# A hybrid encoder layer on one core: square sums spread between dense matmul steps, four small moves beside it

## The chip, the core and the metric

The kernel runs on one core of a Trainium2 chip. A core has a matmul engine (TensorE, PE in the profile), a vector engine (VectorE, DVE), an activation engine (ScalarE, ACT), GpSimd (POOL), and a queue engine that starts DMAs (SyncE, SP). Each runs its own list of instructions in order, and they wait for one another through semaphores. On-chip memory is SBUF; TensorE writes to PSUM, which has eight banks here. The metric is the device time of one execution in microseconds (us); lower is better.

## The reference

One layer (DEPTH = 1) of a streaming encoder is applied to a prompt of 1024 frames and to 32 further frames of another stream, 1024 channels wide, all in 32-bit floats:

```
xn = rmsnorm(x, g_mix)
u_lru, y_lru, q, k, v, gates = split(xn @ w_in)
xc = causal_dwconv(u_lru)                   # width 4
h  = rg_lru(xc)                             # two block-diagonal gates, then a scan over positions
br_lru  = (h * gelu(y_lru)) @ w_br_lru
q, k = rmsnorm(q per head, g_q), rmsnorm(k per head, g_k)
br_attn = attention(q, k, v, sink) @ w_br_attn   # chunks of 64 frames, own chunk and 2 before it
g = sigmoid(gates + b_gate)
x = x + (g0 * br_lru + g1 * br_attn) @ w_out
gate_pre, up = split(rmsnorm(x, g_ffn) @ w_up)
x = x + (gelu(causal_dwconv(gate_pre)) * up) @ w_down
```

Outputs are x for both streams and the states: last inputs of the convolutions, last h, last keys and values.

## The kernel before

Activations lie transposed, channels on the 128 partitions and the T = 1056 frames (1024 + 32) along the free dimension, as KT = 8 rows of 128 channels. The frames are cut into three chunks of 352. A dense product (`chunk`) is a run of 8 **steps**, one for each k; a step is three matmuls of 128x352 (high part of the weights by high part of the data, high by low, low by high: three passes in a fast format stand for one in full precision). A tile is 3 chunks by 8 steps, 72 matmuls. Tiles go in pairs, X in PSUM banks 0 to 2 with weight slot 0 and Y in banks 3 to 5 with slot 1. SyncE loads the next 512 KB of weights when a tile is done, and GpSimd splits them into high and low parts. The order of the work on each engine is written out by hand, so TensorE's list below is the program's.

The stages in order: the norm and the first tiles; keys; values; attention, in two halves of 17 blocks (the 16 chunks of frames and the sample's); attention's output product; the recurrent part (`PAIR_R`), one row of 128 channels for each turn of a loop; the gated product with its result (`PAIR_G0`); the output product; the feed-forward part in three thirds; the stores of the result.

*Keys and values.* Heads are normalised by the sums of squares over 64 channels. For keys, `key_sum` is a matmul of 128x352 in full precision into bank 6 or 7, and ScalarE takes the root (`key_root`, L892). There are six of them, two rows by three chunks, placed in `keys_between` among the steps of a query tile. Values are computed by frames, in nine tiles of 128 frames (`v_half`), each in two halves of 4 steps, whose matmuls are 128x256. Only tiles 0 to 5 have a bank at once; 6 to 8 take the banks of 0 to 2 when ScalarE has copied those out (`v_out`, L896). Queries of two tiles are copied and squared by ScalarE in `last_queries` (L883, L884) while the values are computed.

*Queries' square sums.* `query_sums(a, b)` computes for one half a (0 or 1) the sums of a chunk of frames b: one or two units, and each unit is a full-precision matmul with a 128x128 piece of squares as the stationary operand and a moving operand of 2 columns (L526). A half has 33 units, and the profile records each as two instructions. Half 0 is done in three groups of 12, 12 and 9 units behind the first halves of value tiles 6, 7 and 8 (`SUMS_AT`), half 1 in three groups of the same sizes in attention blocks 13, 14 and 15, between `scores` and `product`.

*Attention.* Block g on TensorE is `scores(g + 1)` (L549), `product(g - 1)` (L575), `transposes(g)` (L560) and then some steps of a dense tile that has nothing to do with it (`fill`): a query tile of half 1, then from block 12 on tiles of the attention's gate, 7 steps for a block. ScalarE does the exponentials (L910), VectorE the maxima, the scaling (L1298), and the copies.

*Recurrent part and what follows it.* For a row j, `lru_gates(j, n)` are two full-precision matmuls of chunk n (L715, L716). ScalarE makes them decays (L1047 to L1054), VectorE scans over the frames and leaves the result of a row as c_hi, d_lo. The last row's three `lru_gates` stand in and before the Y tile of pair `PAIR_G0`. Then comes the X tile of pair `PAIR_G0 + 1`, which multiplies all eight rows by w_br_lru, and which waits at its last step (k = 7) of each chunk for the last row. VectorE joins a finished chunk of it with the gate in GG (L1470, L1473), and ScalarE puts the next gate into GG (L1008), which frees the bank of the Y tile.

*The end.* The last dense tile adds to `resid` (L1569), and SyncE stores each row of 128 channels once its three chunks are done (L396): eight stores of 528 KB, one for each row.

Of the kernel before, what the change touches and what calls it, by code (L numbers as in the profile page):

```python
# [122 lines left out]
def build(nc, xT, W, wab, vecs, mats, kc, vc, yT, o_lconv, o_h, o_fconv, o_kp, o_ks, o_vp, o_vs):  # L123
    ctx = ExitStack()
    with ctx:
# [204 lines left out]
        SUMS_AT = {NB - 4: range(0, 6), NB - 3: range(6, 12), NB - 2: range(12, NB)}  # L330
# [35 lines left out]
        def _(sp):  # L366
# [64 lines left out]
        def _(pe):  # L431
# [29 lines left out]
            def last_row(sem_, value):  # L461
# [4 lines left out]
                return before  # L466
# [43 lines left out]
            def v_half(tt, s):  # L510

                t0 = tt * P if tt < SEQ // P else T - P
                to = bank[tt % 6]
                for k in range(4 * s, 4 * s + 4):
                    for j, (w, x) in enumerate(((w_hi, x_hi), (w_hi, x_lo), (w_lo, x_hi))):
# [4 lines left out]
            def query_sums(a, b):  # L520

                for u in range(units_of(b)):
                    t0 = SMP if b == NC else b * CHUNK + u * DSEQ
                    sq = q_sq[a][:, t0:t0 + DSEQ, :].rearrange("p t r -> p (t r)")
                    at = SUMS_COL[a] + 2 * (2 * b + u)
                    last = nc.tensor.matmul(bank[SUMS_BANK[a]][:, at:at + 2], sq, bones[:, 0:P:HD], start=True, stop=True)  # L526
                if b == NC:
                    last.then_inc(a_qs, 1)
# [50 lines left out]
            def beside(s, p, n, ks):  # L579
# [10 lines left out]
                chunk(s, n, x_hi, x_lo, to=n, ks=ks)  # L590

            def fill(work):
                for (s, p, n), ks in work:
                    beside(s, p, n, ks)

# [40 lines left out]
            key_sum(1, 2)  # L636

            pe.wait_ge(wx_ready, PAIR_V + 1)
            for tt in range(6):
                pe.wait_ge(*((x_act, out_before(2) + tt + 1) if tt < 3 else (y_act, out_before(2) + tt - 2)))  # L640
                v_half(tt, 0)
            pe.wait_ge(wy_ready, PAIR_V + 1)
            for tt in range(3):
                v_half(tt, 1).then_inc(v_done, 1)
            pe.wait_ge(h_rt, 6)
            for tt in range(6, 9):
                pe.wait_ge(v_free, tt - 5)
                v_half(tt, 0).then_inc(x_done, 1)
                if tt == 6:
                    pe.wait_ge(h_sqd, 12)  # L650
                for b in SUMS_AT[tt - 6 + NB - 4]:
                    query_sums(0, b)
# [13 lines left out]
            fill(fill_of(0)[1:])  # L666
            for g in range(1, BLOCKS):
# [4 lines left out]
                if g in SUMS_AT:  # L672
                    pe.wait_ge(x_act, out_before(PAIR_G))
                    pe.wait_ge(y_act, out_before(PAIR_G))
                    for b in SUMS_AT[g]:
                        query_sums(1, b)
                product(g - 1)
                transposes(g)
                fill(fill_of(g))
# [11 lines left out]
            def gated(p0, stage, between=None, second=None, before=None):  # L691
# [4 lines left out]
                if between is not None:  # L696
                    between()
                tile(1, 0, p0, x_hi, x_lo, y_act, ya, before=second)
                pe.wait_ge(x_act, xa + 3)
                if before is not None:  # L700
                    pe.wait_ge(r_lo, START + 3 * (KT - 1))
                tile(0, 0, p0 + 1, c_hi, d_lo, before=before)
# [23 lines left out]
            def gates_first():  # L726
                pe.wait_ge(s_wab, 16 * KT)
                lru_gates(KT - 1, 0)

            def gates_later(n, k):  # L730
                if (n, k) in ((0, KT // 2), (1, 0)):
                    lru_gates(KT - 1, n + 1)


            gated(PAIR_G0, "G0", gates_first, gates_later, last_row(r_lo, START + 3 * (KT - 1)))


# [56 lines left out]
        def _(act):  # L794
# [882 lines left out]
```

## Time and profile before

| | |
|---|---|
| median of 3 runs | 1806.59 us (1802.4, 1808.53, 1806.59) |
| profiled execution, its time | 1809.89 us |
| its span in the trace | 1808.1 us |
| TensorE busy | 1794.6 us, 99% of the span |
| VectorE, ScalarE, GpSimd busy | 838.0, 561.4, 499.8 us |
| mean DMA rate | 49 GB/s |

The span is what the trace covers from the first instruction to the last; the execution's own time is 1.8 us more. A busy TensorE is not one at its peak: its instructions are counted as busy whatever they do and at whatever clock. The page's row PEclk shows the clock that TensorE was granted in 40 equal slices, in tenths.

### The profile page before, as it was taken

The page shows a single profiled execution, that of the slowest core. Times are in us where ns is not written, and L with a number is a line of the kernel's source. Part 1 is how long each engine was busy: PE and PEld are TensorE (multiplying, and loading weights), DVE is VectorE, ACT ScalarE, POOL GpSimd, SP SyncE. Part 2 cuts the span into 40 slices and gives each one's busy share as a digit, 9 for nine tenths or more (in the row PEclk, how much of TensorE's full clock was granted, in tenths as well). Part 3 has the DMA queues.
Part 4 walks back from the last instruction along what each step waited for, and adds up shares of the span by engine and source line. Part 5 has one row for each costly group of instructions (what it writes and reads, how often), then busy time and mean ns, then how long its engine had stood idle before and what let it go on. Part 6 is the DMA issues. An engine that isn't in the chain of part 4 may idle for free.

```text
span 1808.1 us, 29895 instructions
## 1 busy us (share of the span) xinstructions
PE 1794.6 (99%) x11252; PEld 1746.7 (97%) x11252; DVE 838.0 (46%) x1624; ACT 561.4 (31%) x1117; POOL 499.8 (28%) x282
## 2 busy tenths in 40 slices
PE   9999999999999999999999999999999999999999
PEld 8998888899999999999999999999999999999999
DVE  7946757711247676112465555411555511555511
ACT  5535544400156765112133332200322300333300
POOL 3112101122332232333332333332223333333222
PEclk9989989999999999999999999999999999999999
DMA  4011000011111111111311111111111111111113
GB/s 162 25 30 42 24 24 24 24 50 46 39 47 41 52 38 38 47 46 46 143 47 36 46 46 46 47 46 47 46 46 42 41 46 46 46 46 46 46 46 121
DMA packets 28514, 89.16 MB, mean 49 GB/s; under 512 B 3472, under 2 KB 8496, under 8 KB 28464
## 3 DMA queue, kind: packets, MB, share of 16 engines
q1 hardware_dynamic: 25200, 82.49, 13.7%
q10 hardware_dynamic: 3264, 5.96, 1.0%
q8 instruction: 37, 0.61, 0.1%
q14 instruction: 13, 0.11, 0.0%
HBM read 83.70 MB, written 4.73 MB: 49 GB/s over the span
## 4 chain that ended last, share of the span: by engine, by line
PE 95%; DVE 2%; ACT 2%; issue 0%; DMA 0%; SPq 0%; ACTq 0%; DVEq 0%
PE banks L440 85%; PE banks L560 2%; PE banks L575 2%; PE banks L516 1%; PE banks L549 1%; PE banks L526 1%; PE banks L716 1%; PE banks L715 1%; DVE x_lo L1198 1%; DMA resid<-xT 0%; DVE x_lo L1183 0%; DVE resid L1191 0%; ACT prB L910 0%; DVE merged L1206 0%; DVE prB L1298 0%
## 5 line engine op out<-in xcount | busy, mean ns | idle before, releaser
L440 PE MATMUL banks<-x_hi,w_hi 128*128 128x352 f32 x1752 | 578.5, 330 | 4.6 <-DVE x_lo L1183 3.1
L440 PE MATMUL banks<-x_hi,w_lo 128*128 128x352 f32 x1752 | 568.5, 324 | 0.0
L440 PE MATMUL banks<-x_lo,w_hi 128*128 128x352 f32 x1752 | 566.8, 324 | 0.0
L409 POOL TENSOR_SCALAR w_hi<-w_raw 128x1024 fp32r<-128x1024 f32 x137 | 157.0, 1146 | 1238.4 <-DMA w_raw<-W 1238.4
L440 PE MATMUL banks<-h_hi,w_lo 128*128 128x352 f32 x1152 | 372.7, 323 | 0.0
L440 PE MATMUL banks<-h_hi,w_hi 128*128 128x352 f32 x1152 | 372.4, 323 | 0.0
L440 PE MATMUL banks<-h_lo,w_hi 128*128 128x352 f32 x1152 | 371.6, 323 | 0.0
L440 PEld LDWEIGHTS banks<-x_hi,w_hi 128*128 128x128 f32 x1752 | 331.6, 189 | 9.0 <-issue 3.1
L411 POOL TENSOR_TENSOR w_lo<-w_raw,w_hi 128x1024 fp32r<-128x1024 f32 x137 | 334.1, 2439 | 11.4
L440 PEld LDWEIGHTS banks<-x_lo,w_hi 128*128 128x128 f32 x1752 | 331.1, 189 | 2.9
L440 PEld LDWEIGHTS banks<-x_hi,w_lo 128*128 128x128 f32 x1752 | 330.5, 189 | 0.0
L440 PEld LDWEIGHTS banks<-h_hi,w_lo 128*128 128x128 f32 x1152 | 216.6, 188 | 0.0
L440 PEld LDWEIGHTS banks<-h_lo,w_hi 128*128 128x128 f32 x1152 | 216.6, 188 | 0.0
L440 PEld LDWEIGHTS banks<-h_hi,w_hi 128*128 128x128 f32 x1152 | 216.6, 188 | 0.0
L1145 ACT ACT_TABLE_LOAD x24 | 30.8, 1283 | 447.2 <-DVE GB L1542 447.2
L1546 DVE SCALAR_TENSOR_TENSOR GC<-GB,vec,GC 128x352 f32<-128x352 f32 x144 | 138.1, 986 | 65.6 <-ACT GC L1145 60.3
L1569 DVE TENSOR_TENSOR resid<-resid,banks 128x352 f32 x72 | 37.5, 521 | 233.6 <-PE banks L440 233.6
L440 PE MATMUL banks<-c_hi,w_hi 128*128 128x352 f32 x384 | 124.0, 323 | 0.5 <-DVE d_lo L1445 0.5
L440 PE MATMUL banks<-c_hi,w_lo 128*128 128x352 f32 x384 | 124.4, 324 | 0.0
L440 PE MATMUL banks<-d_lo,w_hi 128*128 128x352 f32 x384 | 123.8, 323 | 0.0
L1535 DVE TENSOR_TENSOR GB<-banks,rbc 128x352 f32<-128x352 f32 (+1 forms) x96 | 39.1, 430 | 180.4 <-PE banks L440 179.9
L440 PEld LDWEIGHTS banks<-c_hi,w_hi 128*128 128x128 f32 x384 | 72.3, 188 | 0.8 <-DVE d_lo L1445 0.8
(212 smaller groups left out, 1819.7 us busy)
## 6 DMA issues: line engine op xcount, KB each, us to landing
w_raw<-W SPq DMA_DIRECT2D x139, 512.0 KB, 3.4
resid<-xT SPq DMA_DIRECT2D x6, 704.0 KB, 9.8
sqsum<-xT ACTq DMA_DIRECT2D x2, 2112.0 KB, 13.4
o_yT<-resid SPq DMA_DIRECT2D x8, 528.0 KB, 4.6
wabs<-wab ACTq DMA_DIRECT2D x8, 128.0 KB, 2.0
w_early<-W SPq DMA_DIRECT2D x1, 512.0 KB, 3.7
mat<-mats SPq DMA_DIRECT2D x1, 192.0 KB, 10.1
vec<-vecs SPq DMA_DIRECT2D x1, 143.0 KB, 2.3
```

The source lines that it names most:

```text
L409: nc.gpsimd.tensor_scalar(w_hi[s][:, :], w_raw[s][:, :], 1.0, 0.0, ALU.mult, ALU.add).then_inc(w_hi_done, 1)
L411: nc.gpsimd.tensor_tensor(w_lo[s][:, :], w_raw[s][:, :], w_hi[s][:, :].bitcast(F32), ALU.subtract).then_inc(ready, 1)
L440: last = nc.tensor.matmul(out[:, 0:cn], w[s if wt is None else wt][:, k * P:(k + 1) * P], x[:, k, cc:cc + cn], start=(k == 0 and j == 0), ...
L516: last = nc.tensor.matmul(to[:, 0:2 * P], x[:, k, t0:t0 + P], w[s][:, (k % 4) * 2 * P:(k % 4 + 1) * 2 * P], start=(k == 0 and j == 0), sto ...
L526: last = nc.tensor.matmul(bank[SUMS_BANK[a]][:, at:at + 2], sq, bones[:, 0:P:HD], start=True, stop=True)
L549: last = nc.tensor.matmul(bank[4 + e][:, u * 192:u * 192 + n], q, kG[a][rows, lo:lo + n], start=True, stop=True)
L560: last = nc.tensor.transpose(bank[6 + i][0:kn, v * P:v * P + P], pr_of(b)[:, v, c0:c0 + kn], ident)
L575: last = nc.tensor.matmul(bank[3][64 * e:64 * e + 64, 0:n], v, pt[0:kn, i, e * n:e * n + n], start=(i == 0), stop=(i == len(groups) - 1))
L1145: A(GC[n][:, 0:cn], GB[:, FFN_HIST + c0:FFN_HIST + c0 + cn], ACT.Identity, bias=VD("fconv_b", ft), scale=VD("fconv_w", ft * 3 + 2)).then_i ...
L1535: last = D.tensor_tensor(GB[:, FFN_HIST + g0:FFN_HIST + g0 + cn], bank[n][:, off:off + cn], rbc[:, c0 + off:c0 + off + cn], ALU.mult)
L1546: ins = D.scalar_tensor_tensor(GC[n][:, 0:cn], GB[:, tap + c0:tap + c0 + cn], VD("fconv_w", ft * 3 + tap), GC[n][:, 0:cn], ALU.mult, ALU.add)
L1569: D.tensor_tensor(row(resid, i * 2 + s, c0, cn), row(resid, i * 2 + s, c0, cn), bank[3 * s + n][:, 0:cn], ALU.add).then_inc(free, 1)
```

## The change

1. `query_sums` no longer takes a chunk of frames but a step of a number of steps, and issues the units that fall to it, 1 or 2 of 33 for each of 24 steps in half 0. They stand ahead of every step of the second halves of value tiles 0 to 2 and of the first halves of 6 to 8. The waits for the squares and for the key roots move ahead of value tile 0's second half.
2. For half 1 they stand ahead of the steps of the filling tile in blocks 12, 13 and 14, from the third step of each block on: 5 steps in a block, 11 units (2 or 3 for a step).
3. The key sums of chunk 2 of row 0 and those behind it stand half a chunk further on, one at a time; the last comes after value tile 1.
4. ScalarE copies value tile 6 before the first exponentials and not after them.
5. The last row's `lru_gates` stand at steps (0, 2), (0, 6) and (1, 2) of the Y tile, where they stood before it, at (0, 4) and at (1, 0). The X tile after it does steps 0 to 6 of all three chunks, and then step 7 of each, where it did chunk after chunk.
6. The last output row is stored in three pieces, one for each chunk.

The diff, cut to its core:

```
-        SUMS_AT = {NB - 4: range(0, 6), NB - 3: range(6, 12), NB - 2: range(12, NB)}
+        UNITS, SUMS_STEPS = 2 * NC + 1, 24
+        SUMS_BLOCKS, SUMS_FROM = (NB - 5, NB - 4, NB - 3), 2
...
-            for k in range(KT):
+            for k in range(KT - 1):
                 sp.wait_ge(x_dve if k % 2 == 0 else y_dve, ...)
                 sp.dma_start(yT[k], resid[:, k, 0:T]).then_inc(s_out, 16)
-            sp.wait_ge(s_out, 16 * (6 + 3 + KT))
+            for n, (c0, cn) in enumerate(CHUNKS):
+                sp.wait_ge(y_dve, Y_END - 2 + n)
+                sp.dma_start(yT[KT - 1, :, c0:c0 + cn], resid[:, KT - 1, c0:c0 + cn]).then_inc(s_out, 16)
+            sp.wait_ge(s_out, 16 * (6 + 3 + KT + 2))
...
+            def query_sums(a, step, steps):
+
+                for i in range(step * UNITS // steps, (step + 1) * UNITS // steps):
+                    t0 = SMP if i == UNITS - 1 else i * DSEQ
                     sq = q_sq[a][:, t0:t0 + DSEQ, :].rearrange("p t r -> p (t r)")
+                    at = SUMS_COL[a] + 2 * i
...
+            def fill_with_sums(g):
+
+                at, steps = 0, sum(len(ks) for _, ks in fill_of(g)) - SUMS_FROM
+                first = steps * SUMS_BLOCKS.index(g)
+
+                def before(k):
+                    nonlocal at
+                    if at == SUMS_FROM:
+                        pe.wait_ge(a_lo, g)
...
+                    if at >= SUMS_FROM:
+                        query_sums(1, first + at - SUMS_FROM, steps * len(SUMS_BLOCKS))
+                    at += 1
+                for (s, p, n), ks in fill_of(g):
+                    beside(s, p, n, ks, before)
...
-                elif (n, k) == (1, 0):
+                elif (n, k) == (1, 4):
                     key_sum(0, 2)
+                elif (n, k) == (2, 0):
                     key_sum(1, 0)
-                elif (n, k) == (2, 0):
+                elif (n, k) == (2, 4):
                     key_sum(1, 1)
...
-                tile(0, 0, p0 + 1, c_hi, d_lo, before=before)
+                for n in range(3):
+                    chunk(0, n, c_hi, d_lo, ks=range(KT - 1))
+                for n in range(3):
+                    chunk(0, n, c_hi, d_lo, last_row(r_lo, START + 3 * (KT - 1), n), ks=range(KT - 1, KT))
...
             query_root(0)
+            v_out(6)
             act.wait_ge(h_rdy, 6)
             exps(0)
-            for tt in range(6, 9):
+            for tt in range(7, 9):
                 v_out(tt)
```

TensorE's order before, at value tiles 6 and 7 (`mat` is the table with the two columns of ones, `sqsum` the squares):

```order
L516 MATMUL banks<-w_hi_62,x_hi 128x256 [waits v_freed,heads_norm_root]
...
L526 MATMUL banks<-mat,sqsum 128x2 [waits heads_squared]
L526 MATMUL banks<-mat,sqsum 128x2 x11
L516 MATMUL banks<-w_hi_62,x_hi 128x256 [waits v_freed]
...
L526 MATMUL banks<-mat,sqsum 128x2 x12
```

And now, from the first step of value tile 6:

```order
L532 MATMUL banks<-mat,sqsum 128x2 [waits v_freed,heads_norm_root]
L522 MATMUL banks<-w_hi_62,x_hi 128x256
L522 MATMUL banks<-w_hi_62,x_lo 128x256
L522 MATMUL banks<-w_lo_61,x_hi 128x256
L532 MATMUL banks<-mat,sqsum 128x2 x2
L522 MATMUL banks<-w_hi_62,x_hi 128x256
```

Runs of 12 units with nothing between them are now runs of one or two, with the three matmuls of a step between them.

TensorE's order before in the X tile of pair `PAIR_G0 + 1`, from the last step of its chunk 0 (`c_hi`, `d_lo` are the rows of the recurrent part; the semaphore lru_lo counts them):

```order
L440 MATMUL banks<-c_hi,w_hi_62 128x352 [waits lru_lo]
L440 MATMUL banks<-d_lo,w_hi_62 128x352
L440 MATMUL banks<-c_hi,w_lo_61 128x352
L440 MATMUL banks<-c_hi,w_hi_62 128x352
L440 MATMUL banks<-d_lo,w_hi_62 128x352
```

And now, from the last step of chunk 0 to the start of the Y tile behind it:

```order
L444 MATMUL banks<-c_hi,w_hi_62 128x352 [waits lru_lo]
L444 MATMUL banks<-d_lo,w_hi_62 128x352
L444 MATMUL banks<-c_hi,w_lo_61 128x352
L444 MATMUL banks<-c_hi,w_hi_62 128x352 [waits lru_lo]
...
L444 MATMUL banks<-x_hi,w_hi_65 128x352 [waits y_freed_by_act,wy_ready]
L444 MATMUL banks<-x_lo,w_hi_65 128x352
```

Chunk 0's last step was followed by chunks 1 and 2, 16 steps; it is now followed by two steps and then by the Y tile, which waits for ScalarE.

## Rows read from the trace of the kernel before

**Rows 1.** The page: granted clock in 40 slices; DMA issues, us to landing last:

```profile
PEclk9989989999999999999999999999999999999999
...
w_raw<-W SPq DMA_DIRECT2D x139, 512.0 KB, 3.4
```

**Rows 2.** Waits of TensorE over the span: total us, times, longest:

```profile
PE banks L508 <- ACT merged L892: 1.5, 1, 1.5
PE banks L440 <- ACT vtok L896: 1.4, 1, 1.4
PE banks L715 <- ACT FI L1048: 0.9, 1, 0.9
PE banks L440 <- DVE d_lo L1445: 0.5, 1, 0.5
```

**Rows 3.** Windows: stretch, length, busy us (PE, PEld, DVE, ACT, POOL), PEclk, DMA:

```profile
109.60:126.70 17.10, 17.10 (x83) 17.10 (x82) 0.00 (x0) 0.38 (x1) 3.43 (x2) 0.50 0.10 32
226.00:229.20 3.20, 3.20 (x15) 3.20 (x14) 2.19 (x6) 2.66 (x11) 0.00 (x0) 0.50 0.00 0
...
246.20:249.60 3.40, 3.40 (x16) 3.40 (x15) 1.82 (x4) 3.12 (x9) 0.00 (x0) 0.51 0.00 0
```

**Rows 4.** Timeline of TensorE, first sums: start us, us, what:

```profile
106.32 2.73 PE L526 MATMUL banks<-mat,sqsum 128*128 128x2 f32 x24
109.12 0.28 PE L516 MATMUL banks<-w_hi,x_lo 128*128 128x256 f32 x1
...
130.18 0.66 PE L549 MATMUL banks<-merged,sqsum 64*128 64x64 f32 x8
```

**Rows 5.** Timeline of TensorE, attention blocks 12 and 13:

```profile
216.49 1.09 PE L560 MATMUL banks<-mat,prA 128*128 128x128 f32 x8
217.34 0.40 PE L440 MATMUL banks<-x_hi,w_hi 128*128 128x352 f32 x1
...
220.89 0.92 PE L549 MATMUL banks<-merged,sqsum 64*128 64x192 f32 x8
...
225.53 1.80 PE L560 MATMUL banks<-mat,prB 128*128 128x128 f32 x8
226.98 0.64 PE L440 MATMUL banks<-x_hi,w_hi 128*128 128x352 f32 x1
...
231.52 0.92 PE L549 MATMUL banks<-merged,sqsum 64*128 64x192 f32 x8
```

**Rows 6.** Timeline of TensorE, nine like sums in the second norm:

```profile
969.20 2.06 PE L752 MATMUL banks<-mat,nacc 128*128 128x2 f32 x18
...
971.38 0.33 PE L440 MATMUL banks<-h_lo,w_hi 128*128 128x352 f32 x1
```

**Rows 7.** Timeline of TensorE where the values begin:

```profile
92.23 0.28 PE L516 MATMUL banks<-w_hi,x_lo 128*128 128x256 f32 x1
92.35 0.28 PE L516 MATMUL banks<-w_lo,x_hi 128*128 128x256 f32 x1
```

**Rows 8.** Timeline of ScalarE: first square of the last queries:

```profile
94.97 0.85 ACT L884 ACTIVATE sqsum<-banks 128x352 f32<-128x352 f32 x1
```

**Rows 9.** Timeline of TensorE, VectorE, ScalarE at the join of chunk 1:

```profile
718.48 0.32 PE L440 MATMUL banks<-c_hi,w_lo 128*128 128x352 f32 x1
718.84 0.52 DVE L1470 SCALAR_TENSOR_TENSOR GV<-GG,banks 128x352 f32<-128x352 f32 x1 [2.58 <-PE banks L440]
719.49 0.56 ACT L1008 ACTIVATE GG<-banks,halfb 128x352 f32<-128x352 f32 x1 [1.99 <-DVE GV L1470]
722.49 0.32 PE L440 MATMUL banks<-x_hi,w_hi 128*128 128x352 f32 x1
```

**Rows 10.** Timeline of ScalarE ahead of the first new gate:

```profile
715.65 1.28 ACT L1008 ACT_TABLE_LOAD   x1 [1.36 <-DVE GV L1470]
```

**Rows 11.** DMA issues near the end: queue, count, KB, us to landing:

```profile
o_yT<-resid SPq DMA_DIRECT2D x1, 528.0 KB, 2.6
o_h<-st_h SPq DMA_DIRECT2D x1, 8.0 KB, 2.8
```

More of the change, by code:

```diff
@@ L459, in loop_tiles, with last_row @@
                     tile(1, i, p0, hiy, loy, fy, i * 3 + y0)
-            def last_row(sem_, value):
+            def last_row(sem_, value, chunk_=None):
                 def before(n, k):
@@ L465, in before @@
                         pe.wait_ge(sem_, value + (n + 1))
-                return before
+                return before if chunk_ is None else lambda k: before(chunk_, k)
             def norm_sums(n):
@@ L514, in v_half @@
                 for k in range(4 * s, 4 * s + 4):
+                    if sums is not None:
+                        query_sums(0, sums + k - 4 * s, SUMS_STEPS)
                     for j, (w, x) in enumerate(((w_hi, x_hi), (w_hi, x_lo), (w_lo, x_hi))):
@@ L577, in product, with beside @@
                 last.then_inc(a_O, 1)
-            def beside(s, p, n, ks):
+            def beside(s, p, n, ks, before=None):
                 if ks[0] == 0:
@@ L589, in beside, with fill @@
                         pe.wait_ge(y_act, out_before(p) + n - 2)
-                chunk(s, n, x_hi, x_lo, to=n, ks=ks)
-            def fill(work):
-                for (s, p, n), ks in work:
+                chunk(s, n, x_hi, x_lo, before, to=n, ks=ks)
+            def fill(g):
+                for (s, p, n), ks in fill_of(g):
                     beside(s, p, n, ks)
+            def fill_with_sums(g):
[5 more added lines that the diff above has]
+                        pe.wait_ge(a_lo, g)
+                        if g == SUMS_BLOCKS[0]:
+                            pe.wait_ge(x_act, out_before(PAIR_G))
+                            pe.wait_ge(y_act, out_before(PAIR_G))
+                    if at >= SUMS_FROM:
+                        query_sums(1, first + at - SUMS_FROM, steps * len(SUMS_BLOCKS))
+                    at += 1
+                for (s, p, n), ks in fill_of(g):
+                    beside(s, p, n, ks, before)
             pe.wait_ge(wx_ready, 1)
@@ L635, in _ @@
             tile(1, 0, 2, x_hi, x_lo, y_act, out_before(2), before=keys_between)
-            key_sum(1, 2)
             pe.wait_ge(wx_ready, PAIR_V + 1)
@@ L647, in _ @@
                 pe.wait_ge(v_free, tt - 5)
[L648 to L652, printed above, removed]
+                v_half(tt, 0, 4 * (tt - 3)).then_inc(x_done, 1)
             for tt in range(3, 6):
@@ L665, in _ @@
             beside(s, p, n, ks[6:])
-            fill(fill_of(0)[1:])
+            for (s, p, n), ks in fill_of(0)[1:]:
+                beside(s, p, n, ks)
             for g in range(1, BLOCKS):
@@ L671, in _ @@
                     pe.wait_ge(a_lo, g - 1)
[L672 to L676, printed above, removed]
                 product(g - 1)
                 transposes(g)
-                fill(fill_of(g))
+                if g in SUMS_BLOCKS:
+                    fill_with_sums(g)
+                else:
+                    fill(g)
             pe.wait_ge(a_lo, BLOCKS - 1)
@@ L689, in _, with last_gates, gated @@
             loop_tiles(PAIR_B + 1, KT // 2 - 1, c_hi, d_lo, c_hi, d_lo, x_dve, X_DVE["B"] + 3, y_dve, Y_DVE["B"] + 3)
-            def gated(p0, stage, between=None, second=None, before=None):
+            def last_gates(n, k):
+                if (n, k) == (0, 2):
+                    pe.wait_ge(s_wab, 16 * KT)
+                    lru_gates(KT - 1, 0)
+                elif (n, k) in ((0, 6), (1, 2)):
+                    lru_gates(KT - 1, n + 1)
+            def gated(p0, stage):
                 xa, ya, xd = X_ACT[stage], Y_ACT[stage], X_DVE[stage]
                 tile(0, 0, p0, x_hi, x_lo, x_act, xa)
-                if between is not None:
-                    between()
-                tile(1, 0, p0, x_hi, x_lo, y_act, ya, before=second)
+                tile(1, 0, p0, x_hi, x_lo, y_act, ya, before=last_gates)
                 pe.wait_ge(x_act, xa + 3)
-                if before is not None:
-                    pe.wait_ge(r_lo, START + 3 * (KT - 1))
-                tile(0, 0, p0 + 1, c_hi, d_lo, before=before)
+                pe.wait_ge(r_lo, START + 3 * (KT - 1))
+                pe.wait_ge(wx_ready, p0 + 2)
+                for n in range(3):
+                    chunk(0, n, c_hi, d_lo, ks=range(KT - 1))
+                for n in range(3):
+                    chunk(0, n, c_hi, d_lo, last_row(r_lo, START + 3 * (KT - 1), n), ks=range(KT - 1, KT))
                 tile(1, 0, p0 + 1, x_hi, x_lo, y_act, ya + 3)
```

24 lines of the change are left out of this document (9 added, 15 removed).

## The prediction

> **What bounds the kernel now.** I read the page's first part first. TensorE is busy for 1794.6 us of a span of 1808.1, so an edit counts only by what it takes from TensorE's list: a wait, or time in which its work runs slowly. The waits come next: all of TensorE's that the table of waits shows within the stages of the change are four, 1.5, 1.4, 0.9 and 0.5 us [rows 2]. Then the row PEclk: it has an 8 in the third and in the seventh slice [rows 1]. Windows over those slices show where: from 109.6 to 126.7 us the granted clock was 0.50 (1.2 GHz), and three more times in attention blocks 13 to 15 for about 3.4 us each (the first and the last of three stand in [rows 3]). TensorE is busy in all of them, so no wait shows this loss. What stood ahead of each fall, the timeline tells: a run of square sums, two columns wide, 2.73 us long [rows 4] and as long before the falls at 225.8 and 236, somewhat shorter before the last.
>
> **Sums of half 0.** A run of 24 instructions (12 units) begins at 106.32, and the second matmul behind it at 109.12, one pace of 0.12 us (92.23 to 92.35, [rows 7]) after the first, so 12 units cost 2.68 us at full clock, 0.223 each. From 106.32 to the scores at 130.18 TensorE does 33 units and six half tiles of 12 matmuls: 33 x 0.223 + 72 x 0.119 = 7.4 + 8.6 = 16.0 us with no clock lost. It took 23.9 [rows 4]. So 7.8 us are the slow clock's. Nothing is removed by the change: it issues the same 33 units and the same matmuls. Does a unit alone between dense matmuls cost more than one of twelve? The trace shows nine in a run between dense matmuls: 971.38 - 969.20 = 2.18, less one pace of 0.16, is 2.02 or 0.224 a unit [rows 6]. Nine and twelve cost the same per unit, so entering and leaving a run costs nothing, and I take 0.223 for one alone. No row shows one alone. As bounds I take 0.1 us more or less for each of the 39 places where units now stand (about one instruction of a run, 0.11): +-4 us over both halves.
>
> **Does the clock hold?** It fell after runs of 2.7 us. It didn't after the nine sums of 2.0 us that stand between dense tiles [rows 6], nor round the waits of 1.5 and 1.4 us at 80.5 and 134 [rows 2], which all fall in slices with a 9. In half 0 a step is now 0.36 us of dense matmuls and on average 33/24 units, 0.31 us: somewhat under half of the time is sums, and never more than 0.45 us at a stretch. In half 1 it is 0.48 of dense and 2.2 units, 0.49 us: half. That is nearer to the cases in which TensorE kept 2.4 GHz than to a run of 2.7 us, and I take it that the clock holds: -7.8 us. The wait for the squares moves ahead of value tile 0's second half, at about 100 us; ScalarE has those squares behind it when it begins the last queries, ahead of 95 us [rows 8], so it costs nothing.
>
> The Trainium skill's page "TensorE: Matmul & The Clock Gate", Part 4, says that a transpose on TensorE doesn't count as busy for the clock the way other matmuls do. By that rule the falls in attention would be the transposes' as much as the sums', and this change would leave them where they are. The trace speaks against it: each of the 33 blocks has transposes, and the clock fell only in the three that have sums.
>
> **Sums of half 1.** Block 12 has no sums: 3.55 us from its first dense matmul to the next scores (217.34 to 220.89), and 0.85 for the transposes (216.49 to 217.34). Block 13, after a run: 4.54 and 1.45 [rows 5]. So a fall costs 0.99 + 0.60 = 1.6 us, and three cost 4.8. The units themselves only move. Their new wait on att_lo at the third step comes 1 us after that value was there in block 12 in the profile; behind it on TensorE stands the whole block, but ScalarE and VectorE have a block's time to spare. ScalarE's root over these sums (two table loads) stands where it did and finds its sums earlier. -4.8 us.
>
> **Key sums.** The wait of 1.5 us is for a root on ScalarE; half a chunk later it is past, and a key sum costs the same 0.6 us alone as in a pair. But 1.2 us of that come back: value tile 3 needs a bank whose square ScalarE ends at 94.97 + 0.85 = 95.8 [rows 8], and that chain hangs on VectorE's key norm, not on TensorE. Tile 3 starts at 92.11 + 3 x 1.43 = 96.4 now [rows 7]. It can't start before 95.9. So -0.5 us, with bounds of 0 and -1.7.
>
> **Value tile 6.** The first query tile of half 1 waits 1.4 us for a copy that stands behind the first exponentials. Copied before them it is there some 2.5 us ahead. The exponentials wait for scores that come after the same value tile, so the copy lies in their wait. What is late next? Weights: with the clock held, these matmuls come 8 us sooner after the DMA that feeds them is issued; the DMA takes 3.4 us [rows 1] and GpSimd's two passes 3.6 by the means on the page, 7.0 together, and TensorE gets there six half tiles of 1.43 and the scores of 0.8 later, 9.4 us. The wait goes: -1.4 us.
>
> **Recurrent part.** Here the change puts a wait in place of one. The first gates move behind six dense matmuls, 1 us. ScalarE would start their decay 0.55 us later, which shifts its chain: the wait of 0.9 for FI shrinks to about 0.5. The wait of 0.5 for d_lo (with the gap before the matmul 0.75) goes, for the X tile reaches step 7 six microseconds later. -1.15 us together. But now chunk 0 ends only two steps, 0.96 us, before the Y tile wants to start, and the Y tile's first bank is freed by ScalarE's gate, which needs VectorE's join of chunk 0. From the start of a chunk's last matmul to the join is 718.84 - 718.48 = 0.36, to the gate 0.65 more, the gate itself 0.56 [rows 9]; before this first one stands a table load of 1.28 behind the join [rows 10]. Sum 2.85 + 0.1 for the semaphore, against 0.16 + 0.96 = 1.12 us that TensorE has until then (paces of (722.49 - 718.48)/25 = 0.16 [rows 9]). A new wait of 1.8 us. In the kernel before, 16 steps (7.7 us) lay between, which hid it all. Net +0.65 us.
>
> **The last store.** The last DMA carries a third of 528 KB. The 528 KB landed in 2.6 us; 8 KB took 2.8 [rows 11]. By the small store nothing is won, by the bytes at the rate of some 400 GB/s at most 0.9. I take 0.5. "DMA: Bandwidth & Descriptors" of the Trainium skill, section "Anatomy of one DMA", gives about 2.0 us that don't depend on size plus bytes by 436 GB/s: 0.8 us less by that, inside the same bounds. -0.5 us.
>
> **Sum.** -7.8 - 4.8 - 0.5 - 1.4 + 0.65 - 0.5 = -14.35 us. Against the profiled execution's 1809.9 that is 1795.5. Its time is 3.3 above the median of the runs shown, 1806.6, and I set the gain against the median: 1792.2 us. Its own range, with +-4 for the single units, 1.2 for the keys, 0.5 for the store and 2 for the runs' spread: 1787 to 1798.
>
> **Rivals.**
> - *Slower: the clock falls in the mixed stretches and stays down.* It decides where TensorE's clock goes to 1.2 GHz once in a mixed stretch: the rest of the stretch then runs at half speed. For it: at 116 to 122 us the clock stayed at 0.50 though 12 dense matmuls stood between two runs of sums [rows 3, 4]. Against it: that was at a clock already fallen. Price: half 0's stretch, 8.6 + 7.4 = 16 us, doubles, +16 instead of +7.8; half 1's 15 steps of 0.97 us add up to 14.6 instead of 4.8. With -1.75 of the rest: 1806.6 + 8.2 + 9.8 - 1.75 = 1823 us.
> - *The clock holds in half 0 but not in half 1,* where the sums are denser: one to three falls stay, and 1.6 to 4.8 us with them: 1794 to 1797, or some more where a fall lasts longer than now.
> - *The sums aren't the cause in attention* (the page's rule on transposes): 1792.2 + 4.8 = 1797.
> - *The new wait of the Y tile isn't there* (the table already loaded): 1.8 us less, 1790.4.
>
> **Chances.** Forecast 0.72 (with the last rival's 0.05 in it), half 1 falls 0.14, transposes 0.04, slower 0.07, something else 0.03. Ranges of the first three lie between 1787 and 1799. The measurement tells 0.3%, 5.4 us, from no change: faster (below 1801.2) 0.89, the same 0.04, slower 0.07.
>
> **What the profile of the changed kernel would show.** PEclk 9 in both slices and a granted clock of 1.00 from 100 to 125 and 210 to 240 us. The first scores some 10 us earlier than 130.18. Runs of L532 of two or four instructions at 0.11 us each. No wait for vtok, none for merged at 80 us, but one of about 1 us at value tile 3. A wait of TensorE for ScalarE's GG of some 1.8 us behind the X tile of pair `PAIR_G0 + 1`. The forecast is wrong if the clock is 0.50 anywhere past 20 us, or if a unit alone costs over 0.3 us.

## The result and the profile after

The changed kernel takes 1794.88 us (median of 4 runs, 1794.54 to 1795.1), the kernel before took 1807.56 beside it (1802.4 to 1810.41): ratio 0.9933, interval 0.991 to 0.9956. Six later runs of the changed kernel gave 1795.21 (1794.46 to 1796.49) against 1807.25 for 17 of before, ratio 0.9931 (0.9916 to 0.9947). The profiled executions took 1809.89 and 1795.10 us, 14.8 apart.

The page of the changed kernel (busy us of each engine; granted clock in 40 slices):

```profile
PE 1781.3 (99%) x11252; PEld 1733.8 (97%) x11252; DVE 847.7 (47%) x1624; ACT 561.7 (31%) x1117; POOL 500.6 (28%) x282
...
PEclk9999999999999999999999999999999999999999
```

TensorE has as many instructions as before, 11252, and is busy 13.3 us less. No slice has an 8; before, the third and the sixth had one [rows 1] (the prediction's "seventh" is a miscount: its windows at 226 to 250 us lie in the sixth). The windows over the two stretches with sums (columns as in [rows 3]) show a granted clock of 1.00 in both:

```profile
99.90:121.70 21.80, 21.80 (x190) 21.73 (x188) 10.37 (x17) 2.52 (x7) 1.17 (x2) 1.00 0.07 26
208.00:236.00 28.00, 28.00 (x215) 25.22 (x214) 15.96 (x41) 11.56 (x37) 3.43 (x2) 1.00 0.01 2
```

TensorE's timeline shows a unit alone, then two together, and later the first scores of blocks 0, 1 and 17; under it the last two of these before, whose first is in [rows 4]:

```profile
100.15 0.28 PE L532 MATMUL banks<-mat,sqsum 128*128 128x2 f32 x2
100.29 0.36 PE L522 MATMUL banks<-w_hi,x_hi 128*128 128x256 f32 x1
...
100.72 0.28 PE L532 MATMUL banks<-mat,sqsum 128*128 128x2 f32 x2
...
101.30 0.50 PE L532 MATMUL banks<-mat,sqsum 128*128 128x2 f32 x4
...
102.10 0.28 PE L532 MATMUL banks<-mat,sqsum 128*128 128x2 f32 x2
...
121.77 0.66 PE L555 MATMUL banks<-merged,sqsum 64*128 64x64 f32 x8
...
128.31 0.71 PE L555 MATMUL banks<-merged,sqsum 64*128 64x128 f32 x8
...
236.58 0.66 PE L555 MATMUL banks<-merged 64*128 64x64 f32 x8
```

```profile
138.38 0.72 PE L549 MATMUL banks<-merged,sqsum 64*128 64x128 f32 x8
...
251.89 0.66 PE L549 MATMUL banks<-merged 64*128 64x64 f32 x8
```

A step with one unit takes 100.72 - 100.15 = 0.57 us and a step with two 102.10 - 101.30 = 0.80, so a second unit adds 0.23; the step's three matmuls take 0.36, which leaves 0.21 for a unit alone. That is the 0.22 of a unit in a run. The first scores come 8.4 us earlier, those of block 1 10.1, those of block 17 (the first block of half 1) 15.3.

TensorE's waits (total us, times, longest), which stand against [rows 2]:

```profile
PE banks L444 <- ACT GG L1033: 1.8, 1, 1.8
...
PE banks L522 <- ACT sqsum L908: 0.9, 1, 0.9
...
PE banks L748 <- ACT FI L1073: 0.5, 1, 0.5
```

The waits for merged, vtok and d_lo are gone. Two are new: the one for sqsum at value tile 3, and the one for GG. The timeline of the three engines at the Y tile, against [rows 9, 10]:

```profile
705.77 0.52 DVE L1495 SCALAR_TENSOR_TENSOR GV<-GG,banks 128x352 f32<-128x352 f32 x1 [1.88 <-PE banks L444]
706.47 1.28 ACT L1033 ACT_TABLE_LOAD   x1 [5.48 <-DVE GV L1495]
707.77 1.45 ACT L1033 ACTIVATE GG<-banks,halfb 128x352 f32<-128x352 f32 x3
708.47 0.40 PE L444 MATMUL banks<-x_hi,w_hi 128*128 128x352 f32 x1 [1.77 <-ACT GG L1033]
```

The chain is the forecast one: join, table load behind the join's semaphore, gate, matmul. The last pieces of the store landed in 1.8 us instead of 2.6 [rows 11]:

```profile
o_yT<-resid SPq DMA_DIRECT2D x2, 176.0 KB, 1.8
```

### The profile page after: what moved, and what is told of

It reads as the page before. It is cut to its first block, busy times and chain, and to the rows that moved or that the text cites. A ratio compares the mean times of both kernels' runs of the same rounds, so it can differ in the third digit from the quotient of the medians.

```text
span 1793.3 us, 29900 instructions
## 1 busy us (share of the span) xinstructions
PE 1781.3 (99%) x11252; PEld 1733.8 (97%) x11252; DVE 847.7 (47%) x1624; ACT 561.7 (31%) x1117; POOL 500.6 (28%) x282
## 4 chain that ended last, share of the span: by engine, by line
PE 95%; DVE 3%; ACT 1%; DMA 0%; issue 0%; SPq 0%; ACTq 0%; DVEq 0%
PE banks L444 87%; PE banks L566 2%; PE banks L581 2%; PE banks L555 1%; PE banks L522 1%; PE banks L748 1%; PE banks L749 1%; PE banks L532 1%; DVE x_lo L1223 1%; DVE sqsum L1231 0%; DMA resid<-xT 0%; DVE merged L1231 0%; DVE x_lo L1208 0%; ACT sqsum L958 0%; DVE resid L1216 0%; DVE prB L1323 0%
## 5 line engine op out<-in xcount | busy, mean ns | idle before, releaser
L1594 DVE TENSOR_TENSOR resid<-resid,banks 128x352 f32 x72 | 37.5, 521 | 233.7 <-PE banks L444 233.7
## 6 DMA issues: line engine op xcount, KB each, us to landing
mat<-mats SPq DMA_DIRECT2D x1, 192.0 KB, 10.1
```

Of the source, the lines that this page charges most:

```text
L1594: D.tensor_tensor(row(resid, i * 2 + s, c0, cn), row(resid, i * 2 + s, c0, cn), bank[3 * s + n][:, 0:cn], ALU.add).then_inc(free, 1)
```

## The experiments

All kernels are the changed one with the edit shown. Its own time, 1795.2, is the base. The runs came on three chips, on which the kernel before took 1807.3, 1807.1 and 1807.3 us, so the base serves for all three. A stretch at 0.50 of the clock is called a spell below. Ten of the fourteen profiles have one that begins before 15 us too, and an execution's start differs (the first scores of undisturbed profiles came at 120.8 to 122.4), so what is smaller than some 2 us is read inside one trace, from one instruction to another.

**Half 0's sums in groups again.**

```
-                v_half(tt, 0, 4 * (tt - 3)).then_inc(x_done, 1)
+                v_half(tt, 0).then_inc(x_done, 1)
+                sum_units(0, 12 * (tt - 6), min(12 * (tt - 5), UNITS))
```

> The changed kernel with half 0's 33 sums back in groups of 12, 12 and 9 behind the first halves of value tiles 6, 7 and 8; everything else as changed. Theory (a run of sums 2.7 us long brings the clock down, and it stays at 0.50 until 126): +7.8 us over the changed kernel, 1802.7 us; granted clock 0.50 again from the first group to about the scores, first full scores 8.4 us later than 121.77. Rival (the clock fell for another reason, and the gain came from moved waits): the clock stays 1.00, +0 to 1 us.

1800.42 (1799.13 to 1803.11, 10 runs): +5.2. In its trace the clock was at 0.50 in one stretch:

```profile
113.17:123.41 10.24, 10.24 (x51) 10.24 (x50) 0.00 (x0) 0.43 (x2) 3.42 (x2) 0.50 0.15 53
```

From value tile 3 to the first scores TensorE takes 30.7 us here and 26.0 in the changed kernel: the 10.24 us cost 4.7, and the 17.1 of before [rows 3] cost 7.8, both 0.46 of their length and not half. Two of the groups, from the same timeline:

```profile
105.53 2.73 PE L536 MATMUL banks<-mat,sqsum 128*128 128x2 f32 x24
109.64 2.73 PE L536 MATMUL banks<-mat,sqsum 128*128 128x2 f32 x24
```

The first passed without a fall, and the spell came 1 us after the end of the second. So it is shown that the groups bring the falls, but a run of 2.7 us does so in some cases and not in all: the same groups cost 7.8 us in the profile of before and 4.7 in this one.

**Half 1's sums in groups again.**

```
+                if g in SUMS_BLOCKS:
...
+                    n = 12 * SUMS_BLOCKS.index(g)
+                    sum_units(1, n, min(n + 12, UNITS))
                 product(g - 1)
...
-                    fill_with_sums(g)
+                fill(g)
```

> The changed kernel with half 1's sums back in groups of 12, 12 and 9 ahead of the products of attention blocks 13 to 15. Theory: three falls of the clock of some 3.4 us, 1.6 us each, +4.8 us, 1799.7 us. Rival (half 0's falls brought these with them, or the transposes' company did it together with other work that the change moved): no fall, 1794.9 us.

1802.18 (1799.91 to 1803.89, 10 runs): +7.0, more than forecast. The edit wasn't quite what its text says: `SUMS_BLOCKS` begins at block 12, so the groups stood one block earlier than before the change. Its timeline and windows:

```profile
205.46 4.04 PE L536 MATMUL banks<-mat,resid 128*128 128x2 f32 x24 [0.74 <-ACT resid L914]
```

```profile
206.79:213.62 6.83, 6.83 (x32) 5.69 (x32) 0.70 (x2) 2.16 (x9) 3.39 (x2) 0.50 0.02 8
220.45:223.86 3.41, 3.41 (x16) 2.29 (x16) 0.42 (x1) 1.39 (x6) 0.00 (x0) 0.50 0.00 0
230.69:234.10 3.41, 3.41 (x17) 2.48 (x14) 0.44 (x2) 1.91 (x8) 0.00 (x0) 0.50 0.00 0
```

In block 12 the last squares are late, a wait of 0.74 stands right ahead of the first group, and the first spell is twice as long. 0.74 + 13.65 / 2 = 7.6 us; from the scores of block 1 to those of block 17 the trace shows 7.5 more (115.7 against 108.3). The transposes alone as a cause are out: the changed kernel has them all at 1.00.

**The same groups in the middle of the dense steps.**

```
-                    if at >= SUMS_FROM:
-                        query_sums(1, first + at - SUMS_FROM, steps * len(SUMS_BLOCKS))
+                    if at == SUMS_FROM:
+                        n = 12 * SUMS_BLOCKS.index(g)
+                        sum_units(1, n, min(n + 12, UNITS))
```

> The changed kernel with half 1's sums in groups of 12, 12 and 9 in attention blocks 13 to 15, as before the change, but in the middle of the block's dense steps (ahead of its third step) and not beside product and transposes. Theory (a run of sums 2.7 us long brings the clock down wherever it stands): two to four spells at 0.50, +3 to +8 us over the changed kernel's 1794.9, about as with the groups ahead of the products (1802.2 median, 1799.9 to 1803.9). Rival (it takes sums, products and transposes together, a stretch with few dense matmuls; surrounded by dense matmuls the same run is harmless): no spell, 1794.9.

1797.04 (1794.63 to 1800.7, 10 runs), +1.8, in blocks 12 to 14 too. In the profiled execution one spell came, at the end of the group of 24 instructions that ran from 216.42 to 219.3; the other two groups had none, and half 1 took 1.4 us more than in the changed kernel:

```profile
218.90:222.31 3.41, 3.41 (x14) 3.41 (x14) 0.00 (x0) 0.00 (x0) 0.00 (x0) 0.50 0.02 5
```

Neither theory holds whole: dense steps on both sides make falls fewer without making the run safe. How much of the difference to the groups ahead of the products is due to their neighbours isn't shown, since there the wait of 0.74 stood ahead of the first group as well, and here none does.

**Half 0 in three lumps** with eight dense steps between two of them.

```
+                        if step % 8 == 0:
+                            n = 12 * (step // 8)
+                            sum_units(0, n, min(n + 12, UNITS))
```

> The changed kernel with half 0's sums in three lumps of 12, 12 and 9 units ahead of steps 0, 8 and 16 of the 24: the share of sums over the whole stretch is the changed kernel's (7.4 of 16 us), only the length of a run (2.7 us) is that of before, and 2.9 us of dense matmuls stand between two runs instead of 1.4. Theory run length (a run of 2.7 us is enough to lower the clock): falls after at least two of the three lumps, +1.5 to +6 us. Rival share (only the mean over the stretch counts): no fall, +0 us, 1794.9.

1798.71 (1796.49 to 1801.24, 7 runs), +3.5; spells in its trace:

```profile
102.04:108.87 6.83, 6.83 (x34) 6.83 (x34) 6.65 (x10) 0.73 (x2) 0.00 (x0) 0.50 0.00 0
112.28:115.69 3.41, 3.41 (x19) 3.41 (x18) 0.00 (x0) 0.38 (x1) 0.00 (x0) 0.50 0.00 0
```

The same units and the same dense steps as in the changed kernel, and the clock fell. So the mean over the whole stretch doesn't decide.

**Half 0 in six lumps** of 5 or 6 units, one ahead of every fourth step.

```
+                        if step % 4 == 0:
+                            query_sums(0, step // 4, 6)
```

> The changed kernel with half 0's sums in six lumps of 5 or 6 units (1.1 to 1.3 us) ahead of every fourth step, each followed by 1.43 us of dense matmuls: the same share over the stretch as in the changed kernel and as with three lumps of 12, 12 and 9 (1798.7 median, 1796.5 to 1801.2). Theory (the share counts over a few us, so alternation every 1.3 us is fine enough): no spell at 0.50, 1794.9 +-0.5. Rival (any run longer than the changed kernel's 0.45 us risks a fall): 1796 to 1801, different from run to run.

1795.88 (1794.27 to 1796.59, 5 runs), no spell past 20 us in its trace, and 26.0 us from value tile 3 to the first scores as in the changed kernel. Runs of 1.0 to 1.3 us with 1.4 us of dense work between are as good as single units, within the measurement. Over what time a share would count, as the theory has it, no run here shows.

**Every unit of half 0 twice.**

```
+                    for _ in range(2 - a):
                         last = nc.tensor.matmul(bank[SUMS_BANK[a]][:, at:at + 2], sq, bones[:, 0:P:HD], ...)
```

> The changed kernel with each of half 0's units computed twice, one behind the other, at the same places: 66 units of 0.223 us, 14.7 us, beside 8.6 us of dense matmuls, so sums fill 0.63 of the stretch in runs of at most four units (0.9 us). If the clock holds: +33 x 0.223 = +7.4 us, 1802.3 us. If a share of over half lowers the clock although each run is short: the stretch of 23.3 us is at 0.50 for at least one spell, +9 to +25 us.

1819.89 (1819.81 to 1820.27, 4 runs), +24.7. Its timeline and the windows round the fall:

```profile
103.88 0.50 PE L533 MATMUL banks<-mat,sqsum 128*128 128x2 f32 x4
104.68 1.00 PE L533 MATMUL banks<-mat,sqsum 128*128 128x2 f32 x8
106.33 0.85 PE L533 MATMUL banks<-mat,sqsum 128*128 128x2 f32 x4
...
136.84 1.70 PE L533 MATMUL banks<-mat,sqsum 128*128 128x2 f32 x8
```

```profile
100.00:105.40 5.40, 5.40 (x51) 5.40 (x49) 5.26 (x7) 0.38 (x1) 0.00 (x0) 1.00 0.01 3
105.50:142.90 37.40, 37.40 (x177) 37.40 (x177) 3.92 (x9) 1.16 (x3) 0.00 (x0) 0.50 0.04 14
```

No run is longer than 1 us at full clock, and the clock fell at 105.4 and stayed down for 37.5 us, up to some 4 us past the last unit. The stretch from value tile 3 to the first scores takes 50.8 us against 26.0, 24.8 more: 7.4 for the units and 17.4 for the clock, again 0.46 of the spell. This is the slower rival of the prediction, with its mechanism as written (down once, down for the rest of the stretch). The changed kernel is on the good side of it; one with twice as many sums isn't.

**Wide units in groups again**, for both halves (half 1's in blocks 12 to 14, as above).

```
-                    ... bank[SUMS_BANK[a]][:, at:at + 2], sq, bones[:, 0:P:HD], ...
+                    ... bank[SUMS_BANK[a]][:, at:at + P], sq, bones.rearrange("p (e j) -> p j e", e=2), ...
```

> The changed kernel with the sums of both halves back in their groups of 12, 12 and 9 at the old places (each half alone so cost 5.5 and 7.3 us, both together would be about 1807), but each unit's moving operand is 128 columns wide instead of 2: the two wanted columns first, then repetitions of them that the next unit writes over, so that the sums come out in the same place. Theory (the clock falls since a unit of two columns leaves the array nearly idle, though TensorE counts as busy): the unit still takes 0.22 to 0.25 us, since its weight loads set its time, and no spell at 0.50 comes: 1795 to 1797 us. Rival (what lowers the clock is the full-precision format, the stationary loads or the run of small instructions as such): the spells stay, 1805 to 1810. Rival (a wide unit takes its 128 columns on top of its loads, 0.2 us more each): no spells, but 66 x 0.2 = +13 us, 1808.

1799.96 (1798.81 to 1801.0, 7 runs). The timeline of the first group, and the window over it:

```profile
105.01 3.44 PE L536 MATMUL banks<-mat,sqsum 128*128 128x128 f32 x24
108.18 0.39 PE L522 MATMUL banks<-w_hi,x_hi 128*128 128x256 f32 x1
```

```profile
105.00:113.00 8.00, 8.00 (x63) 8.00 (x62) 3.74 (x9) 0.00 (x0) 0.00 (x0) 1.00 0.00 0
```

A run of 3.2 us, longer than any of before, and no spell anywhere in this execution; the seven runs had mean clocks of 0.998 to 1.000. Format and stationary loads are those of the groups and the runs are no shorter; what differs is the number of columns, 128 and not two. So none of the first three lowers the clock by itself. The time is 4.8 over the base and so outside the theory's 1795 to 1797. A unit now takes (108.18 - 105.01) / 12 = 0.264, 0.04 more, which is 2.7 us for 66; the wait of 0.74 of block 12 is there too. The rest, about 1.3, was not taken apart.

**The recurrent and gated part as before.**

```
-                if (n, k) == (0, 2):
...
+                if (n, k) in ((0, KT // 2), (1, 0)):
...
+                tile(0, 0, p0 + 1, c_hi, d_lo, before=last_row(r_lo, START + 3 * (KT - 1)))
```

> The changed kernel with the recurrent and gated part as before (first gates of the last row ahead of the Y tile, the next two after 4 and 8 steps; the X tile chunk by chunk with its eighth step in each chunk). Theory (the new wait of 1.8 us costs more than the removed waits of 0.4 and 0.75): this edit alone made the kernel slower by 0.65 to 0.75, so undone it is 1794.2, and TensorE has waits for FI of 0.9 and for d_lo of 0.5, none for GG. Rival (the edit pays, since the d_lo wait is larger once the rest is earlier): 1795.5 to 1796.5.

1794.8 (1793.94 to 1795.97, 5 runs), -0.4, too little for the times alone. Its waits:

```profile
PE banks L743 <- ACT FI L1068: 0.9, 1, 0.9
...
PE banks L444 <- DVE d_lo L1465: 0.5, 1, 0.5
```

Both old waits are back, none for GG. From the Y tile's start (with the gates that stand ahead of it) to the start of TensorE's last matmul it takes 1110.4 us, the changed kernel 1111.0. So this edit of the change lost 0.6: shown within the traces.

**A new order of the X tile's last steps.**

```
+                for n, last in ((0, False), (1, False), (0, True), (2, False), (1, True), (2, True)):
```

> The changed kernel with the last row's steps of the X tile in another order: seven steps of chunk 0, seven of chunk 1, the eighth of chunk 0, seven of chunk 2, the eighth of chunk 1, the eighth of chunk 2. Theory (the wait for GG is the chain join, table load, gate behind chunk 0's end, which now has 9 steps = 4.3 us more): the wait of 1.8 goes, 1793.1, with at most 0.3 for d_lo's first chunk, which VectorE writes from 5.3 us after the tile's start and TensorE wants at 6.8. Rival (the Y tile waits for the gate of chunk 2 or the last joins anyhow, or d_lo comes late): 1794.3 to 1795.

1793.87 (1792.14 to 1794.2, 4 runs), 0.9 under the run above on the same chip. TensorE has no wait for GG, and the same stretch takes 1109.4 us, 1.6 less than in the changed kernel. Its ScalarE loads the table while chunk 2 is computed:

```profile
703.12 1.28 ACT L1034 ACT_TABLE_LOAD   x1 [3.51 <-DVE GV L1496]
704.42 0.56 ACT L1034 ACTIVATE GG<-banks,halfb 128x352 f32<-128x352 f32 x1
```

It has the lowest median of all that ran and the shortest stretch: the theory is shown, 0.2 short of its 1.8; its trace has a wait of 0.2 for weights (w_lo) instead.

**The third gates one step later on top of that.**

```
-                elif (n, k) in ((0, 6), (1, 2)):
+                elif (n, k) in ((0, 6), (1, 3)):
```

> The changed kernel with the X tile's eighth steps in the new order (that alone: 1.6 us from the Y tile's start to the end) and the last row's third gates one step later, after the third step of the second chunk instead of the second (0.48 us), where TensorE waited 0.5 for FI. Theory: both waits go, 2.1 us less than the changed kernel in the same session, about 1792.8. Rival for the second edit (the gates' own chain ends later and the last row's d_lo is late): a wait for d_lo in the X tile takes the 0.5 back, 1793.3.

1795.06 (1793.89 to 1795.42, 6 runs), beside 1795.21 of the changed kernel: no gain that the times show, the rival and worse. The same stretch takes 1110.4 us, 0.6 under the changed kernel but 1.0 over the order alone. The wait for FI went, and this came (waits, then the timelines of GpSimd and VectorE):

```profile
PE banks L444 <- DVE d_lo L1471: 1.6, 1, 1.6
```

```profile
699.92 2.54 POOL L415 TENSOR_TENSOR w_lo<-w_raw,w_hi 128x1024 fp32r<-128x1024 f32 x1
```

```profile
698.41 4.49 DVE L1465 TENSOR_TENSOR FA<-FI,sqsum 128x352 f32<-128x352 f32 x4
702.83 1.38 DVE L1471 TENSOR_TENSOR d_lo<-FA,c_hi 128x352 fp32r<-128x352 f32 x3
```

The four FA instructions take 2.30 us in the changed kernel and with the order alone, where GpSimd's first pass over the weights (w_hi) runs beside the last of them, and 1.46 with the recurrent part as before, where no pass does. The Y tile ended half a microsecond earlier against VectorE's chain, so the next weights came half a microsecond earlier and GpSimd's second pass over them (w_lo) 0.8, and VectorE's third FA instruction fell under that pass (700.13 to 702.80, 2.67 us). With the gates one step earlier the pass met a d_lo instruction (2.72 us for 0.52 in the changed kernel) that had time to spare.

**The three small edits undone together:** key sums, value tile 6's copy, the store.

```
-            v_out(6)
             act.wait_ge(h_rdy, 6)
             exps(0)
-            for tt in range(7, 9):
+            for tt in range(6, 9):
...
-                elif (n, k) == (1, 4):
+                elif (n, k) == (1, 0):
                     key_sum(0, 2)
...
+            for k in range(KT):
```

> The changed kernel with the three small edits undone together: key sums where they were, value tile 6's copy behind the first exponentials, the last row stored in one piece. Each shows at its own place: key sums +0.5 to +0.6 before value tile 3 (a wait for the root of 1.5 comes, the one of 0.9 for the copied queries goes), the copy +1.4 to +1.7 between the two first scores, the store +0.8 behind the last matmul. Sum +2.9, 1797.8 us. Rival for the keys (the 0.9 wait isn't tied to the key sums): +1.5 there, 1798.8. Rival for the copy (with the sums spread, the first exponentials come 8 us earlier against the weights, so the copy isn't late any more): 1796.3.

1799.38 (1797.6 to 1801.8, 7 runs), +4.2 against 2.9 forecast; the profiled execution is 3.4 above that of the changed kernel. Its waits, then VectorE ahead of the first exponentials and GpSimd at the same time:

```profile
PE banks L441 <- ACT vtok L915: 2.5, 1, 2.5
...
PE banks L509 <- ACT merged L911: 1.5, 1, 1.5
```

```profile
122.20 1.95 DVE L1290 TENSOR_SCALAR nrq<-rq 128x66 f32<-128x66 f32 x1
```

```profile
121.70 2.38 POOL L412 TENSOR_TENSOR w_lo<-w_raw,w_hi 128x1024 fp32r<-128x1024 f32 x1
```

The keys are as forecast (wait of 1.5, none for sqsum; +0.6), the store too (+0.8). The copy costs 2.8 between the two first scores and not 1.4: with the sums spread, the first scores meet GpSimd's pass over the weights (121.70 to 124.08), and an instruction of 0.2 us takes 1.95. The changed kernel has the same delay on VectorE:

```profile
121.69 2.32 DVE L1296 TENSOR_SCALAR nrq<-rq 128x66 f32<-128x66 f32 x1
```

But there the copy stands ahead of that chain, and TensorE doesn't wait for it. Of the 2.8, 0.8 comes back by block 17 (107.5 us from the scores of block 1, against 108.3): the next pass of GpSimd stretches a VectorE instruction to 2.26 us at 130.5 in the changed kernel, and none here. That this is the whole 0.8 wasn't taken apart.

**The changed kernel again.**

> The changed kernel once more, beside the others on one chip, as their base: 1794.9 by its four runs so far. By the theory no run of it has a spell at 0.50 past the start, so all its runs should lie within 1 or 2 us, while those of before spread over 10 us, as its groups of sums meet a fall of the clock or don't.

1795.21 (1794.46 to 1796.49, 6 runs): 2.0 us from end to end, before 9.2. But its profiled run, the slowest of the six, has a spell. Windows across the wait for GG (705.8 to 707.6) and behind it:

```profile
705.00:709.00 4.00, 2.23 (x15) 1.96 (x14) 2.85 (x6) 2.73 (x4) 0.00 (x0) 1.00 0.40 131
709.00:712.40 3.40, 3.40 (x14) 3.40 (x13) 0.00 (x0) 0.00 (x0) 2.74 (x2) 0.50 0.00 0
```

That refutes the expectation's "no run" in one case. From the Y tile's start to the last matmul this execution takes 2.3 us more than the other profile of the same kernel: some 1.7 for the spell, and a wait of 0.5 for weights (w_lo). The spell begins 1.4 us after the new wait, and nothing else out of the ordinary stands ahead of it; but ten profiles have that wait and only this one the spell, so that the wait caused it is likely and not shown.

## Why the prediction was right, and where it was off

The steps, from instruction to instruction in the two profiled executions (before, less after):

| step | forecast | measured |
|---|---|---|
| key sums: start of value tile 3 | -0.5 | -0.6 |
| half 0: value tile 3 to the first scores | -7.8 | -7.8 |
| value tile 6: scores of block 0 to block 1 | -1.4 | -1.7 |
| half 1: scores of block 1 to block 17 | -4.8 | -5.2 |
| to the end of pair `PAIR_G0`'s X tile, not touched | 0 | +0.6 |
| recurrent and gated part: to the last matmul | +0.65 | +0.8 |
| store: last matmul to the end | -0.5 | -0.8 |
| sum | -14.35 | -14.8 |

The rows are rounded one by one; the sum is that of the unrounded ones. The stretch that wasn't touched takes 442.0 to 442.7 us in the twelve other profiles of changed kernels, 442.0 in before and 442.5 here; its 0.6 is that spread. That the sum of a profile comes out within 0.4 us is in part luck: half 1, the copy, the store and the key sums gave 1.1 us more than forecast, and that spread and the recurrent part took 0.7 back.

*Half 0, half 1.* Right in mechanism and, for this pair of executions, in size. The unit alone at 0.22 held; the bounds of 4 us for it were far too wide. The argument for the clock was weaker than it reads. It set a run of 2.0 us that passed against runs of 2.7 us that didn't, but the group ahead of the fall at 246.2 had nine units and 2.1 us, and of the runs of 2.6 to 2.7 us at full clock in the experiments some passed. Nor does the wait at 134 us lie in a slice with a 9: it is in the third, with the 8, though outside the spell. The waits "within the stages of the change" leave out one of 1.0 us in attention (for small). And the blocks with transposes are 34, not 33. None of this enters the sum. The first scores came 8.4 us earlier; the steps ahead of them add up to 8.3, and the "some 10" of the prediction's last part fits neither.

*Key sums.* Right, with the wait that came back: value tile 3 starts at 95.77, 0.1 ahead of the earliest that was given, with 0.9 of wait.

*Value tile 6.* The wait went. The text asked what would be late next and named the weights. They weren't; GpSimd's pass over them stretched a VectorE instruction ahead of the first exponentials to 2.3 us, which TensorE didn't feel.

*Recurrent part.* Right, sign and all three waits. What was missed is that such a wait can also cost clock.

*Store.* 0.8 by the trace and by the landing times; taken was 0.5. The Trainium skill's "DMA: Bandwidth & Descriptors", section "Anatomy of one DMA", states its figures for DMAs that GpSimd issues, while SyncE issues these; 0.8 is the estimate by them. The trace agrees with that difference, 528 KB in 2.6 us and 176 in 1.8, but not with the times themselves, which the same figures put at 3.2 and 2.4, an estimate too.

*The base: the step that failed.* The sum against the profiled execution gives 1795.5, and the changed kernel's profiled execution took 1795.1. "I set the gain against the median" took 3.3 us off again, and 1792.2 is 2.7 too low. From median to median the gain is 12.7 us, and 14.35 was forecast. The gain wasn't the same in every execution. The kernel before varies with its spells at 0.50: of its 22 runs beside the first experiments, the fastest, 1801.54, had a mean granted clock of 0.997, the slowest two, 1810.97 and 1811.46, 0.990 and 0.991. The profiled one had 0.992 and much slow clock; the change takes away just that. From a typical execution it takes some 12 us, from this one 14.8. A gain that consists of a disturbance belongs to the execution in which it was read.

*The rivals.* The slower one doesn't hold for the changed kernel but is real: twice the sums bring it. Its price was put too high, since it counts double time for what runs at 0.50, and a spell costs 0.46 of its length here. The one of half 1 (1794 to 1797) didn't come; the time of 1794.9 alone would have fitted it, and only the clock of 1.00 from 208 to 236 us rules it out. The missing table load didn't come either. By the rule on transposes in "TensorE: Matmul & The Clock Gate", Part 4 of the Trainium skill, the falls in attention would have stayed (1797). The trace doesn't bear out that result: 208 to 236 us is at 1.00 with the transposes at their old places, and so is the rest of attention. That a transpose counts for nothing isn't thereby refuted.

## What to carry to other kernels

A busy engine can be slow: read the granted clock beside the busy share, and where a stretch is at half speed, look for long runs of matmuls with few columns ahead of it, spread them between dense steps (lumps of 1.0 to 1.3 us with 1.4 us between did it here), or give them more columns where these are nearly free. Spreading has its limit: twice as many sums in the same places brought the clock down for 37.5 us. If a kernel's time varies by half a per cent from execution to execution, suspect such falls, and set a gain that consists of them against the execution that it was read from. Before moving work by half a microsecond, look at what the other engines do under it, since here it decided whether a GpSimd pass met an instruction with time to spare or one in the chain that TensorE waited for.

## What the runs showed that was not expected

- A unit of 128 columns in full precision takes 0.264 us, one of 2 columns 0.223: the time is nearly the loads'.
- A VectorE instruction that meets GpSimd's subtraction over 128x1024 ended only behind it in these cases: 0.20 us became 1.95, and 0.52 became 2.72. The Trainium skill, "SBUF — State Buffer", section "Who interferes with whom", says that the two engines share a pair of ports: of a VectorE instruction that needs it and one of GpSimd, the one that comes first holds it to its end while the other is blocked. The traces agree: VectorE's instruction ended at 124.15, GpSimd's pass at 124.08.
- With every unit of half 0 doubled the clock stayed at 0.50 for 37.5 us, some 4 us of it in dense matmuls alone behind the last sums; nothing here shows why it came back when it did.
- A spell costs 0.46 of its length in the stretches of half 0, and not half: at 0.50 a dense matmul of the values takes 0.213 us from one to the next, at 1.00 0.119, which is 1.8 times as long and not twice.
- A single wait of 1.8 us of TensorE between dense tiles was followed by a spell at 0.50 in one of the ten profiles that have it.
